# Two-stage transformer block on one core: where the rotation products, the sines and the gates stand in the middle attention stage

## The reference

```python
q = apply_rope(q_d.reshape(bsz, seq, DIFF_HEADS, 2, DIFF_HEAD_DIM), cos, sin)
k = apply_rope(k_d.reshape(bsz, seq, DIFF_HEADS, 2, DIFF_HEAD_DIM), cos, sin)
...
s = jnp.einsum('bqhcd,bkhcd->bhcqk', qi, k).astype(jnp.float32) * scale
p = jax.nn.softmax(jnp.where(mask, s, MASK_VALUE), axis=-1)
w = p[:, :, 0] - lam * p[:, :, 1]          # differential weights
y_d = rmsnorm(w @ v, subln_g) * (1.0 - lambda_init) * jax.nn.silu(g_d)
...
p = jax.nn.softmax(mem_scores, axis=-1)    # memory attention
y_x = (p @ mv) * jax.nn.silu(g_x)
mix = jnp.concatenate([y_s, y_d, y_x], axis=-1) @ w_out[l]
```

## Time and profile before

| | us |
|---|---|
| median of 3 runs | 3012.83 (3012.28 to 3015.34) |
| the profiled execution | 3011.3 |
| its span in the trace | 3009.5 |
| TensorE busy | 2825.9 (94% of the span) |
| VectorE busy | 1517.9 (50%) |
| ScalarE busy | 987.8 (33%) |
| GpSimd busy | 503.3 (17%) |

### The profile page before, as it was taken

How to read it: one execution, slowest core, us unless ns; L and a number is a source line. 1 busy time by engine, 2 the same in 40 slices (tenths; PEclk the granted TensorE clock), 3 DMA queues, 4 the chain that set the end, 5 groups by cost and what they waited for, 6 DMA issues and landing times. The chain is left out here.

```text
span 3009.5 us, 36233 instructions
## 1 busy us (share of the span) xinstructions
PE 2825.9 (94%) x14018; PEld 2228.0 (74%) x14018; DVE 1517.9 (50%) x2057; ACT 987.8 (33%) x1708; POOL 503.3 (17%) x607
## 2 busy tenths in 40 slices
PE   7899999988769999999999999899989999989897
PEld 5666665667447868888888877688878877867785
DVE  6587887867563552125533436423253385546334
ACT  4444444434353333122211126411142232226321
POOL 2544445424341030000000002100010000002000
PEclk9999999999789999999999999999999999999998
DMA  5577787765213242233333341322313444441421
GB/s 189 183 306 304 286 313 290 282 248 175 101 57 126 86 180 83 78 110 134 117 108 131 121 159 64 116 78 96 119 49 107 143 168 147 154 163 60 161 98 56
DMA packets 111687, 447.20 MB, mean 149 GB/s; under 512 B 11440, under 2 KB 19760, under 8 KB 76208
## 3 DMA queue, kind: packets, MB, share of 16 engines
q1 hardware_dynamic: 111536, 445.16, 40.7%
HBM read 375.25 MB, written 69.86 MB: 148 GB/s over the span
## 5 line engine op out<-in xcount | busy, mean ns | idle before, releaser
L2732 PE MATMUL ps<-h_hi,w_hi 128*128 128x512 f32 x1600 | 576.9, 361 | 0.0
L2733 PE MATMUL ps<-h_lo,w_hi 128*128 128x512 f32 x1600 | 565.1, 353 | 0.0
L2734 PE MATMUL ps<-h_hi,w_lo 128*128 128x512 f32 x1600 | 561.4, 351 | 0.0
L389 PE MATMUL ps<-h_hi,w_hi 128*128 128x512 f32 (+1 forms) x1152 | 413.1, 359 | 35.0 <-DVE w_lo L348 35.0
L390 PE MATMUL ps<-h_lo,w_hi 128*128 128x512 f32 (+1 forms) x1152 | 412.1, 358 | 0.0
L391 PE MATMUL ps<-h_hi,w_lo 128*128 128x512 f32 (+1 forms) x1152 | 410.0, 356 | 0.0
L2732 PEld LDWEIGHTS ps<-h_hi,w_hi 128*128 128x128 f32 x1600 | 301.9, 189 | 49.8 <-issue 6.2
L2733 PEld LDWEIGHTS ps<-h_lo,w_hi 128*128 128x128 f32 x1600 | 301.7, 189 | 46.5 <-issue 6.2
L2734 PEld LDWEIGHTS ps<-h_hi,w_lo 128*128 128x128 f32 x1600 | 300.8, 188 | 43.7
L2510 DVE TENSOR_TENSOR w_lo<-raw,w_hi 128x2048 fp32r<-128x2048 f32 x64 | 146.4, 2287 | 310.7 <-ACT w_hi L2413 310.6
L389 PEld LDWEIGHTS ps<-h_hi,w_hi 128*128 128x128 f32 x1152 | 220.0, 191 | 70.1 <-DVE w_lo L348 37.9
(11 more groups left out here) (385 smaller groups left out, 4729.5 us busy)
## 6 DMA issues: line engine op xcount, KB each, us to landing
raw<-w_in SPq DMA_DIRECT2D x112, 1024.0 KB, 5.2
raw<-ada_w SPq DMA_DIRECT2D x96, 1024.0 KB, 8.3
raw<-w_out SPq DMA_DIRECT2D x48, 1024.0 KB, 4.9
proj<-xw SPq DMA_DIRECT2D x60, 384.0 KB, 2.6
xw<-proj SPq DMA_DIRECT2D x72, 256.0 KB, 3.4
xw<-proj SPq DMA_DIRECT2D x46, 384.0 KB, 3.4
xw<-resid SPq DMA_DIRECT2D x8, 1536.0 KB, 11.7
proj<-wide SPq DMA_DIRECT2D x32, 256.0 KB, 10.8
```

Of the source, the lines that this page charges most:

```text
L389: pe.matmul(a_[q], wh, h_hi[:, h0 + k, lo:hi], start=k == 0, stop=False)
L2732: pe.matmul(a_[q], wh, h_hi[:, k, a:b], start=k == 0, stop=False)
L2733: pe.matmul(a_[q], wh, h_lo[:, k, a:b], start=False, stop=False)
L2734: ins = pe.matmul(a_[q], wl, h_hi[:, k, a:b], start=False, stop=k == KC - 1)
```

## The change

- In `glu()`, ScalarE makes the two sines behind block 5's steps and waits there for both angles, instead of at the end of its list.
- In `middle_attention()`, VectorE makes all four products of head 0: x·sin into wt[0] and wt[1] first, then x·cos. The rotation of head 0's queries goes to x_ps, that of its keys to o_ps[1], which is bank 6, so that TensorE needs no add between the two. The values of head 0 are transposed behind scores(0) and scores(1) instead of ahead of them. SyncE waits for the four products before it overwrites q_sb.
- GpSimd no longer has a turn_part(0) and makes turn_part(i + 1) ahead of silu(i) instead of behind it.
- The tanh and the product of the memory heads' gates 4, 5, 6, 7 stand in passes 17, 20, 22, 24 (`silu_at`) instead of 17, 21, 25, 29.

```diff
--- before.py
+++ after.py
@@ -1288,10 +1288,10 @@
                             for z in range(2):
                                 ins = act.activation(fm[l][:, :, z, :], bank(2 + 2 * l + z).rearrange("p (g d) -> p g d", g=4), ACT.Copy)
                             ins.then_inc(y_copied.h, 1)
-                    act.wait_ge(m5.h, m5.at(1))
-                    act.activation(sin1, sin1, ACT.Sin)
-                    act.wait_ge(m5.h, m5.at(2))
-                    act.activation(cos1, cos1, ACT.Sin)
+                        if b == 5:
+                            act.wait_ge(m5.h, m5.at(2))
+                            act.activation(sin1, sin1, ACT.Sin)
+                            act.activation(cos1, cos1, ACT.Sin)
 
                 @block.vector
                 def _(dve):
@@ -1616,6 +1616,8 @@
 
             back = {19: 0, 21: 1, 23: 2, 25: 3}
 
+            silu_at = {17: 4, 20: 5, 22: 6, 24: 7}
+
             with nc.Block() as block:
                 @block.sync
                 def _(sp):
@@ -1625,6 +1627,8 @@
                         sp.dma_start(raw[:, n, :], then(n)).then_inc(raw_full[n].h, 16)
                     for i in range(1, 2 * H):
                         if i < H:
+                            if i == 1:
+                                sp.wait_ge(q_done.h, q_done.at(4))
                             sp.wait_ge(rot_done.h, rot_done.at(2 * i - 1))
                             sp.dma_start(q_sb, proj[16 + i]).then_inc(loaded[0].h, 16)
                             sp.wait_ge(rot_done.h, rot_done.at(2 * i))
@@ -1675,8 +1679,10 @@
 
                     def rotate(i, z):
 
-                        pe.wait_ge(q_done.h, q_done.at(4 * i + 2 * z + 2))
-                        pe.matmul(x_ps, rot[:], (q_sb, k_sb)[z], start=True, stop=True).then_inc(rot_done.h, 1)
+
+                        pe.wait_ge(q_done.h, q_done.at(4 * i + 2 * z + 2 if i else z + 1))
+                        pe.matmul(x_ps if i or not z else o_ps[1], rot[:], (q_sb, k_sb)[z] if i else wt[z], start=True, stop=True
+                                  ).then_inc(rot_done.h, 1)
 
                     def values(i):
                         pe.wait_ge(loaded[2].h, loaded[2].at(16 * (i + 1)))
@@ -1722,12 +1728,10 @@
                         ins.then_inc(turned_back.h, 1)
 
                     rotate(0, 0)
-                    pe.wait_ge(roped.h, roped.at(1))
                     rotate(0, 1)
-                    pe.wait_ge(roped.h, roped.at(2))
-                    values(0)
                     scores(0)
                     scores(1)
+                    values(0)
                     for g in range(UNITS):
                         i, b = divmod(g, 4)
                         if g + 2 < UNITS:
@@ -1763,10 +1767,7 @@
                 @block.gpsimd
                 def _(pool):
                     def turn_part(i):
-
                         for z, (x, dst) in enumerate(((q_sb, qc), (k_sb, kc))):
-                            if i == 0 and z:
-                                continue
                             pool.wait_ge(loaded[z].h, loaded[z].at(16 * (i + 1)))
                             pool.wait_ge(roped.h, roped.at(2 * i + z - 1))
                             pool.tensor_tensor(dst, x, cos1, ALU.mult).then_inc(q_done.h, 1)
@@ -1796,11 +1797,10 @@
                         pool.wait_ge(res_hi.h, res_hi.at(pr + 1))
                         pool.tensor_tensor(h_lo[:, 12 + j, c0:c0 + CT], gate[H + j][:, c0:c0 + CT],
                                            h_hi[:, 12 + j, c0:c0 + CT].bitcast(F32), ALU.subtract)
-                    turn_part(0)
                     for i in range(H):
-                        silu(i)
                         if i + 1 < H:
                             turn_part(i + 1)
+                        silu(i)
                     for j in range(H):
                         scale_rows(j)
                     for pr in range(2 * H):
@@ -1876,8 +1876,8 @@
                             v_out(i + 1)
                         if b == 3 and i + 1 < H:
                             gate_tanh_of(i + 1)
-                        if b == 1 and i >= H:
-                            gate_tanh_of(i)
+                        if g in silu_at:
+                            gate_tanh_of(silu_at[g])
                         if g - 1 in back:
                             high_diff(back[g - 1])
                         if g > D_UNITS + 2 and b % 2:
@@ -1894,7 +1894,7 @@
                         dve.wait_ge(rot_done.h, rot_done.at(n + 1))
 
                         dve.wait_ge(s_ready.h, s_ready.at(4 * (i - 1)))
-                        dve.tensor_tensor(dst, x_ps, (qc, kc)[z], ALU.add).then_inc(roped.h, 1)
+                        dve.tensor_tensor(dst, x_ps if i or not z else o_ps[1], (qc, kc)[z], ALU.add).then_inc(roped.h, 1)
 
                     def peak(g):
                         nk = keys(g)
@@ -1953,12 +1953,13 @@
                         dve.scalar_tensor_tensor(x, o_ps[pr % 2][:, 0:CT], 0.5, x, ALU.mult, ALU.mult).then_inc(res_done.h, 1)
 
                     dve.tensor_scalar(neg_lam, lam[:, 6:7], -1.0, None, ALU.mult).then_inc(st.step(), 1)
-                    dve.wait_ge(loaded[1].h, loaded[1].at(16))
-                    dve.tensor_tensor(kc, k_sb, cos1, ALU.mult).then_inc(st.step(), 1)
-                    dve.wait_ge(st.sem, st.now)
-
-                    dve.wait_ge(q_done.h, q_done.at(2))
-                    dve.tensor_tensor(k_sb, k_sb, sin1, ALU.mult).then_inc(q_done.h, 2)
+
+                    for z, x in enumerate((q_sb, k_sb)):
+                        dve.wait_ge(loaded[z].h, loaded[z].at(16))
+                        dve.tensor_tensor(wt[z], x, sin1, ALU.mult).then_inc(q_done.h, 1)
+                    for x, dst in ((q_sb, qc), (k_sb, kc)):
+                        dve.tensor_tensor(dst, x, cos1, ALU.mult).then_inc(q_done.h, 1)
+                    dve.wait_ge(q_done.h, q_done.at(4))
                     rope(0, 0)
                     rope(0, 1)
                     peak(0)
@@ -1989,8 +1990,8 @@
                             dve.tensor_tensor(factor, factor, inv[:, :, 0], ALU.mult).then_inc(factors.h, 1)
                         if b == 0 and i + 1 < H:
                             rope(i + 1, 1)
-                        if i >= H and b == 1:
-                            silu(i)
+                        if g in silu_at:
+                            silu(silu_at[g])
                         if g in back:
                             result_diff(back[g])
                         if g > D_UNITS + 2 and b % 2:
```

## The result

The changed kernel took 2998.18 us (median of 5 runs, 2995.43 to 3000.48); the kernel before, run beside it on the same chip, 3015.34 us (5 runs, 3012.28 to 3021.37). The ratio on record is 0.9938, with a 95% interval of 0.9924 to 0.9952: 0.62% faster. (The two medians alone give 0.9943, inside the interval.) Put on the 3012.83 us of the runs ahead of the prediction the ratio gives 2994.2 us and the medians 2995.7, where 2994.5 was forecast. The profiled execution took 2995.43 us, its span is 2993.6 us, 15.9 less than before.

A forecast was written before the change was run, and what follows sets the result against it. The order of small steps across engines, not a full engine, was taken to bound the stage; -4.15 - 6.33 - 6.33 + 0.8 - 2.3 = -18.3 us off 3012.8 gave 2994.5 us, range 2990.5 to 3002.5.

The forecast's parts named there:

- Sines earlier: End of the gated unit: sines made behind block 5 are hidden, so the stage starts sooner, -1.73 us.
- a tanh of block 7 later than 770.3: Gated unit, ScalarE: listed among the signs in the new profile that would show the forecast wrong.
- Head 0, and head 1's keys: Stage start: head 1's keys ready at 796.2 instead of 800.35, -4.15 us including the earlier sines.
- The pauses between heads: Heads 2 and 3: rotations no longer wait for GpSimd, 2.5 us instead of 8.83, -6.33 us each.
- VectorE beside GpSimd: Heads 2 and 3: VectorE's two-input SBUF operations wait out GpSimd's products, +0.8 us, bounds 0 and +8.
- Gates in other passes: Memory heads: gates moved to passes 17, 20, 22, 24 save 2.3 us, bounds 0 and -3.
- (a) blocking all along: Heads 1 to 3: GpSimd's products block VectorE's weights, seven more us on the path, 3001.5 us; chance 0.15.
- (b) one pause stays: Heads: head 2's keys land late or GpSimd falls behind, one 6.3 us pause remains, 3000.8 us; chance 0.08.
- (d) TensorE at its lower clock: Whole stage: TensorE stays at clock 0.5 and becomes the bound, +19.6 less 5.1, 3027 us; chance 0.03.
- (c) full clock from head 0 on: Stage: TensorE at full clock with fewer pauses, another 1.4 to 2.5 us off, 2992 to 2993; chance 0.13.

## Why the prediction was right, and where its terms were not

The total came out as forecast, within 0.3 us by the ratio, 1.2 by the medians and 2.4 by the span. The interval of the ratio is +-4 us wide, so this closeness says little; what the trace shows of the change, in the stage and the gap ahead of it, was 14.75 us, 3.5 less than the sum of 18.3, and the terms say more. Undone one at a time, the four parts give 1.72 for the sines, 1.34 for head 0, 11.02 for the order and 0.83 for the passes, 14.9 together, so no large part of the 14.75 is left without a cause.

1. *Sines earlier, -1.73:* -1.71 measured, -1.72 with the edit alone. The forecast had named a tanh of block 7 later than 770.3 as a sign against it; it was at 770.97, but the copy of block 5, which stands ahead of the sines, was 0.72 us later too (762.74 against 762.02), and the tanh waited for TensorE, not for ScalarE's queue. The Trainium skill (ScalarE: Activation LUTs, What ACT_TABLE_LOAD costs) adds a drain of 1.38 us to each load; here the load at 763.39 ends where the sine starts, and the one at 765.84 where the tanh does, so the trace shows 1.28 and nothing else.

2. *Head 0, and head 1's keys, -4.15 with the first:* -3.1. Head 0 itself was right (5.32 us after the start; 5.59 by the forecast's times, 774.05 to 779.64). That head 1 then waits for its transfer was right as well: freeing the transfer moved its keys by 3.9 us. Two sizes were off. The tile landed 0.64 us later behind the start than before; its product started 14.14 to 14.75 us behind the start in the six programs with the changed head 0 and the weights in their place, so this is scatter that the single trace of before couldn't show. And the forecast let the four products, the rotation and the add follow each other in 8.0 us, where 8.38 were needed. The step overlooked: only head 0's keys have a bank of their own. From head 1 on both rotations write the one bank, so the second waits for the first's add, which was then later than the product, as the first rotation ran at the lower clock.

3. *The pauses between heads, twice -6.33:* right, to 0.02 us (8.83 to 2.51, twice). The undone order gave 11.02 us back.

4. *VectorE beside GpSimd, +0.8:* mis-sized; some 2.1. The forecast's one place, L1920 behind head 2's keys, cost 1.09 (1.31 less 0.22). The second, L1907 ahead of them, cost 0.98, which the run with the waiting product confirmed by taking just that away; the row of 790.86 in the trace of before would have shown it. The failed step was the list of what can be held: "VectorE's operations with two inputs in SBUF". The rest of the twelve products fell where VectorE waits for scores anyway, as argued: L1923 took 1.70 us at 798.63 and cost nothing: it ended at 800.33, and the masked scores for the next maxima were done at 800.38. That cover was the lower clock's: the score products there took 2.08 us, and 1.13 at the same place of head 2.
   With both, -12.66 + 0.98 + 1.09 = -10.6, against -5.34 - 5.38 = -10.7 measured.

5. *Gates in other passes, -2.3:* mis-sized, -0.55 from unit 21 to 31 and -0.55 behind them (of which the run with the old passes gives the passes 0.26), while 0.20 was lost ahead of them to TensorE's clock. Most pass lengths were near what was worked out: 3.01, 3.32 and 2.83 for passes with a gate and no result (2.85, 3.1 and 2.85 forecast), 1.71 for a plain pass. But of the three passes with a result behind a gate's two took 2.82 and 2.81, where 2.00 and 2.04 were forecast, as L1927 was held by GpSimd's subtraction. The forecast did name this meeting, gave it 0.1, and thought of the gate's product; it was the scaling of the weights, twice 0.83, and the run without the subtraction found 1.83 us in it. This was the largest error, and the same one as in step 4: the wrong list.

The rivals. *(a) blocking all along* is right in kind: 2.1 in the heads and 1.7 in the passes, some 3.7 us together, 2.8 more than the forecast had for it, where 7 more was its price. *(b) one pause stays* and *(d) TensorE at its lower clock* are out: no rotation of heads 2 and 3 waits for GpSimd, and the clock over the stage rose from 0.80 to 0.86. *(c) full clock from head 0 on* came in part: head 0's scores ran at it (unit 1's four products took 0.70 us, 1.23 before), but it saved nothing, as head 1 waited for its tile; behind that wait both rotations of head 1 took 2.04 and 2.08.

Within the stage all the errors went one way, 3.5 us together. That the time came out on the forecast nevertheless is luck: single executions scatter (2995.43 to 3000.48 us here, and the stage's start, ahead of which ten of the programs are the same, lay between 771.86 and 782.02 us).

## What to carry to other kernels

When two engines feed a third in turns, ask of each moved group of instructions not only whether its own result is in time but which short steps of a neighbour it now covers; a step of 0.17 us that has to wait out one of 1.27 costs more than its own length suggests, and the loss shows as a long bar, not as a wait. In reading a trace, list every short instruction whose length varies between equal instances, and what ran beside the long ones, before naming the rule for what can be held. And measure the length of the stage, from its first instruction to the first one behind it: here this resolved about 1 us in 118, and less between two fixed instructions inside it, where the time of the whole run did not resolve 6.7 in 3000.

## What the runs showed of the hardware

- VectorE's TENSOR_SCALAR with a single input tile in SBUF is held like the ones with two inputs, for tiles of two columns and more: 128x2, 1.15 us instead of 0.17; 128x256, 1.17 and 1.18 instead of 0.35. Each ended 0.03 to 0.16 us behind the end of GpSimd's TENSOR_TENSOR (802.80 and 802.83; 871.97 and 872.13; 877.62 and 877.77). The Trainium skill (SBUF — State Buffer, Who interferes with whom) says so: it lists `tensor_scalar` among the operations that can take the ports shared with GpSimd, and "an exclusive lock" lets the later one wait for the whole instruction. The trace agrees, for tiles as small as two columns. Which of the two started first the records don't tell so finely: L1920 at 814.61 began 0.02 us ahead of the product that it waited out. By that rule the prediction's -2.4 for the gates, less twice 0.83, would have been about -0.7, an estimate.
- Not held in the same places were a TENSOR_SCALAR of a single column (L1911, 128x1, 0.15 us at 872.50, inside GpSimd's L1798 from 871.93 to 872.70), a reciprocal (870.76, 0.16 us, begun 0.05 us behind GpSimd's subtraction), and reductions, copies and adds from PSUM. GpSimd's own operations were mostly 1.26 to 1.27 us, now and then longer: 1.53 at 799.93, beside VectorE's long L1923.
- A change of ScalarE's table costs 1.28 us, with the neighbours directly at both sides, in three loads (773.07 before, 763.39 and 765.84 after).
- TensorE's clock differs in phase between executions: the same eight products of a memory head took 1.06 to 1.91 us, and the step around them 2.64 to 3.85, in programs that are equal there. Head 0's scores were at the full clock in five of the ten programs with the changed head 0 and at the lower one in the other five. What decides it wasn't tried.
